# Two mixers of a float32 block: the convolution's two projections ahead of the gated attention's queries and keys

## What is computed

```python
p = h @ w_in                                     # 1024 columns in, 2064 out
gq, gk, gv, gr, glr, ca, cg, sq, sk, sv = jnp.split(p, offsets, axis=-1)
# gated linear attention, 4 heads: scores with a decay per key feature, chunks of 64 and a state
glog = jax.nn.log_sigmoid(glr @ w_gate2 + b_gate) / 16
attn = jnp.einsum('bhid,bhjd,bhijd->bhij', qn, kn, decay)
# convolution group: 256 channels, 31 causal taps, then a norm over the channels and a silu
u = ca * jax.nn.sigmoid(cg)
y = depthwise_conv(u, conv_w) + conv_b
# window attention, 8 query heads, window 128, then one projection of all three groups
return jnp.concatenate([o_gla, o_conv, o_swa], axis=-1) @ w_out
```

## Time and profile before

| | |
|---|---|
| median of 3 runs | 1483.65 us (1483.37 to 1484.98) |
| the profiled execution, its own time | 1483.47 us |
| its span, first to last instruction | 1481.7 us |
| mean granted PE clock | 0.999 |
| PE busy, DVE, ACT, POOL | 98%, 65%, 50%, 6% |
| first mixer, second mixer (start of units 0 to the end of the output projection) | about 682 to 792 us, 1175 to 1284 us |

### The profile page before, as it was taken

The page is one execution under the profiler, slowest core; times in us unless marked ns, Lnnn a source line. Parts: engine busy times, 40 slices in busy tenths (PEclk is TensorE's granted clock), DMA queues, the critical chain, the costliest instruction groups (busy, mean ns, idle before and its releaser), DMA issues. The chain is left out here.

```text
span 1481.7 us, 21669 instructions
## 1 busy us (share of the span) xinstructions
PE 1452.5 (98%) x9016; PEld 1272.4 (86%) x9016; DVE 962.5 (65%) x1163; ACT 737.5 (50%) x936; POOL 86.8 (6%) x106
## 2 busy tenths in 40 slices
PE   7999999999999999999999999999999999999998
PEld 7999999899988788888887888878888898788886
DVE  6867786678774765646776666457565577766644
ACT  5433863555543544445565444444444467544442
POOL 0000000000000000000630000000000035000000
PEclk9999999999999999999999999999999999999999
DMA  7735465666655476555523755557754462366542
GB/s 253 235 115 170 143 198 183 172 190 183 181 190 190 147 245 208 176 187 142 153 90 119 237 181 189 174 168 227 227 185 164 141 181 100 116 211 189 180 162 94
DMA packets 253461, 259.16 MB, mean 175 GB/s; under 512 B 26659, under 2 KB 217524, under 8 KB 253364
## 3 DMA queue, kind: packets, MB, share of 16 engines
q1 hardware_dynamic: 252480, 255.49, 54.5%
q10 hardware_dynamic: 884, 2.28, 0.5%
HBM read 256.69 MB, written 1.05 MB: 174 GB/s over the span
## 5 line engine op out<-in xcount | busy, mean ns | idle before, releaser
L994 DVE TENSOR_TENSOR w_lo<-raw,w_hi 128x2048 fp32r<-128x2048 f32 x240 | 545.9, 2277 | 334.5 <-ACT w_hi L601 334.3
L601 ACT ACTIVATE w_hi<-raw 128x2048 fp32r<-128x2048 f32 x240 | 456.3, 1901 | 346.2 <-PE psm L1668 151.6
L1668 PE MATMUL stream<-a_hi,w_hi 128*128 128x256 f32 x1072 | 306.7, 286 | 2.8 <-DVE a_lo L1013 1.7
L1668 PE MATMUL stream<-a_lo,w_hi 128*128 128x256 f32 x1072 | 303.8, 283 | 0.0
L1668 PE MATMUL stream<-a_hi,w_lo 128*128 128x256 f32 x1072 | 303.8, 283 | 0.0
L1668 PE MATMUL stream<-w_hi,a_hi 128*128 128x512 f32 (+1 forms) x640 | 243.6, 381 | 8.0 <-DVE w_lo L994 5.7
L1668 PE MATMUL stream<-w_hi,a_lo 128*128 128x512 f32 (+1 forms) x640 | 239.2, 374 | 0.0
L1668 PE MATMUL stream<-w_lo,a_hi 128*128 128x512 f32 (+1 forms) x640 | 238.9, 373 | 0.0
L1668 PEld LDWEIGHTS stream<-a_hi,w_hi 128*128 128x128 f32 x1072 | 206.1, 192 | 4.9 <-issue 3.0
L1668 PEld LDWEIGHTS stream<-a_lo,w_hi 128*128 128x128 f32 x1072 | 206.3, 192 | 0.0
L1668 PEld LDWEIGHTS stream<-a_hi,w_lo 128*128 128x128 f32 x1072 | 206.2, 192 | 0.0
(11 more groups left out here) (285 smaller groups left out, 1662.2 us busy)
## 6 DMA issues: line engine op xcount, KB each, us to landing
raw<-in_ffn_w_up SPq DMA_DIRECT2D x136, 512.0 KB, 5.0
raw<-in_ffn_w_down SPq DMA_DIRECT2D x104, 512.0 KB, 4.4
raw<-in_ffn_w_gate SPq DMA_DIRECT2D x88, 512.0 KB, 3.9
raw<-in_w_in SPq DMA_DIRECT2D x80, 512.0 KB, 4.6
raw<-in_w_out SPq DMA_DIRECT2D x24, 512.0 KB, 4.2
raw<-in_w_ret_o SPq DMA_DIRECT2D x8, 512.0 KB, 4.1
raw<-in_w_lru_o SPq DMA_DIRECT2D x8, 512.0 KB, 3.9
diag<-in_conv_diag SPq DMA_DIRECT2D x8, 512.0 KB, 5.8
```

The costliest lines, as they stand in the source:

```text
L601: nc.scalar.activation(w_hi[s][:, :, 0:n], raw[s][:, :, 0:n], ACT.Copy).then_inc(w_hi_ready, 1)
L994: V.tensor_tensor(w_lo[s][:, :, 0:n], raw[s][:, :, 0:n], w_hi[s][:, :, 0:n].bitcast(F32), ALU.subtract).then_inc(w_split, 1)
L1668: return nc.tensor.matmul(dst, lhs, rhs, start=start, stop=stop, skip_group_check=True)
```

## The change

In both mixers, on all engines:

- The weights of units 2, 3 and 4 change places: `ca` is now unit 2, `cg` unit 3, queries and keys unit 4. All three have the same size.
- DVE reads `ca` and `cg` first and makes `up`; then come `qg`, `kg` and `qe`, then `conv(0, 2)` and `read_pair(5)`, and only then the drain of tile 0. `lo(cm + 7)` now stands behind this drain.
- ACT takes the tanh of `cg` before `hi(cm + 6)`, four tap products before `hi(cm + 7)` and ten behind it, ahead of `hi(cm + 8)`.
- POOL makes three additions before the key products and the other 25 behind them.
- PE makes the scores of tile 0 behind the whole unit 5, and those of tile 1 behind the whole unit 6 (before: behind their first halves). Of the 21 taps, 7 stand ahead of the cross scores (before 3), then 2, 4, 4, 3 and 1 (before 2, 4, 4, 4 and 4).

No instruction is added or removed.

```diff
@@ SP
-                for n, col in enumerate((0, 784, 1040, 1808)):
+                for n, col in enumerate((784, 1040, 0, 1808)):
@@ POOL
+                sums(0, FIRST_TAPS)
                 for t in range(TT):
-                    pool.wait_ge(group_evac, g_mix + 3)
+                    pool.wait_ge(group_evac, g_mix + 5)
                     pool.wait_ge(e_ready, TT * l + t + 1)
...
-                for n, (f, tap) in enumerate(SUM_TAPS):
...
+                sums(FIRST_TAPS, len(SUM_TAPS))
@@ ACT
+                act.wait_ge(group_evac, gm + 4)
+                nc.scalar.activation(th2[:, :, :], th2[:, :, :], ACT.Tanh, scale=0.5).then_inc(glu_th, 1)
                 hi(cm + 6)
-                act.wait_ge(group_evac, gm + 5)
-                nc.scalar.activation(th2[:, :, :], th2[:, :, :], ACT.Tanh, scale=0.5).then_inc(glu_th, 1)
+                tap_products(0, FIRST_TAPS)
                 hi(cm + 7)
-                tap_products(0, 8)
+                tap_products(FIRST_TAPS, 14)
                 hi(cm + 8)
-                tap_products(8, 14)
@@ DVE
                 sink_columns()
                 lo(cm + 4)
+                read_pair(2, ca[:, :, :], 0.5)
                 lo(cm + 5)
-                read_pair(3, ca[:, :, :], 0.5)
+                read_pair(3, th2[:, :, :], 1.0)
...
+                lo(cm + 6)
+                dve.wait_ge(unit_used, USED[cm + 4])
...
                 for t in range(TT):
-                    dve.wait_ge(group_evac, gm + 3)
+                    dve.wait_ge(group_evac, gm + 5)
...
-                lo(cm + 6)
...
+                conv(0, 2)
+                read_pair(5, sq2[:, :, :], 1.0)
+                gla_scores(0)
                 lo(cm + 7)
-                gla_scores(0)
-                read_pair(5, sq2[:, :, :], 1.0)
-                conv(0, 2)
                 gla_scores(1)
@@ PE
                 unit(5)
                 first_half(5)
+                second_half(5)
                 gla_scores(0)
-                second_half(5)
                 unit(6)
                 first_half(6)
+                second_half(6)
                 gla_scores(1)
-                second_half(6)
...
-                conv_taps(3)
+                conv_taps(7)
                 psm_ready(PSM_CROSS)
...
-                conv_taps(4)
+                conv_taps(3)
                 pe.wait_ge(group_evac, gm + 9)
```

More of the change, by code:

```diff
@@ L86 @@
 HELD = 3
+FIRST_TAPS = 4
 SHARED = (20, 10)
@@ L549, in _, with sums @@
                 nc.gpsimd.memset(up[:, :, 0:TAPS - 1], 0.0).then_inc(zeroed, 1)
+                def sums(first, to):
+                    for n in range(first, to):
+                        f, tap = SUM_TAPS[n]
+                        pool.wait_ge(tap_product, len(SUM_TAPS) * l + n + 1)
+                        if tap:
+                            if tap > 1:
+                                pool.wait_ge(pool_tap, N_SUMS * l + SUM_AT[n])
+                            nc.gpsimd.tensor_tensor(tap_sum[f], tap_sum[f], tap_ring[:, SUM_AT[n] % RING_N, :],
+                                                    ALU.add).then_inc(pool_tap, 1)
+                sums(0, FIRST_TAPS)
                 for t in range(TT):
-                    pool.wait_ge(group_evac, g_mix + 3)
+                    pool.wait_ge(group_evac, g_mix + 5)
                     pool.wait_ge(e_ready, TT * l + t + 1)
@@ L1550, in _ @@
                                        op0=ALU.min, op1=ALU.subtract).then_inc(ps7_free, 1)
[L1551 to L1554, removed]
                 sink_columns()
                 lo(cm + 4)
+                read_pair(2, ca[:, :, :], 0.5)
                 lo(cm + 5)
-                read_pair(3, ca[:, :, :], 0.5)
+                read_pair(3, th2[:, :, :], 1.0)
+                dve.wait_ge(zeroed, 2 * l + 2)
+                dve.wait_ge(group_evac, gm + 3)
+                dve.wait_ge(glu_th, l + 1)
+                V.scalar_tensor_tensor(out=up[:, :, TAPS - 1:TAPS - 1 + T], in0=th2[:, :, :], scalar=1.0,
+                                       in1=ca[:, :, :], op0=ALU.add, op1=ALU.mult).then_inc(up_ready, 1)
+                lo(cm + 6)
+                dve.wait_ge(unit_used, USED[cm + 4])
+                V.scalar_tensor_tensor(out=qg[:, :], in0=bank(4)[:, 0:T], scalar=GDK ** -0.5, in1=rb[:, :],
+                                       op0=ALU.mult, op1=ALU.mult)
+                V.tensor_tensor(kg[:, :], bank(4)[:, T:2 * T], rb[:, :], ALU.mult).then_inc(group_evac, 1)
                 for t in range(TT):
-                    dve.wait_ge(group_evac, gm + 3)
+                    dve.wait_ge(group_evac, gm + 5)
                     dve.wait_ge(e_ready, TT * l + t + 1)
```

## The result

| | before | after |
|---|---|---|
| median | 1483.65 us (7 runs, 1483.36 to 1484.98) | 1490.31 us (7 runs, 1488.91 to 1492.16) |
| the profiled execution, its own time | 1483.47 us | 1490.38 us |
| its span | 1481.7 us | 1488.6 us |
| mean granted PE clock | 0.999 | 0.997 |

The ratio is 1.004, with an interval of 1.003 to 1.005: slower by 6.7 us, where 4.0 were forecast, and past the upper end of the range (1489.4).

The account below looks back on a forecast made before the run. PE was taken to bound the kernel: unchanged work plus waits. Per mixer, +1.8 taps, +0.65 new wait, -0.47 old wait, +0.0 to +0.2 second drain make 2.0; 4.0 in all on 1483.65 us gives 1487.7, range 1485.8 to 1489.4.

Parts of the forecast that it names:

- The chain: From PE's cross scores through ACT, POOL, PE and DVE to `yc`: 36 us whatever PE does, so delay reaches the mean.
- S: How much later the cross scores, and so the convolution's mean, start in each mixer; forecast 1.7 to 2.5 us, chance 0.69.
- Rival 2: The mean does not hang on the cross scores: -0.9 to +0.4 us, 1482.7 to 1484.1 us; chance 0.07.
- S = 2.0: Cross scores at about 735.1 instead of 733.13: +1.8 taps, +0.65 new wait, -0.47 old wait, +0.0 to +0.2 second drain.
- The new wait for `ek`: Before PE's scores of tile 0: PE arrives at 721.2, POOL's key product at 721.8, a wait of 0.65 us.
- The old wait of 0.40: PE's wait for the drain of tile 0, before the scores of tile 1: gone, 0.47 us with its restart.
- The drain of tile 1: DVE's second drain, done at 734.7 or 735.2, about when PE reaches the cross scores: +0.0 to +0.2 us.
- The taps: Seven instead of three ahead of PE's cross scores: four more cost 1.8 us per mixer.
- Turns of DVE and POOL: DVE instructions with two SBUF inputs and POOL's SBUF reads exclude each other: a sum of 4.0 us, 2.4 without turns.
- The sum: Cross scores 2.0 us later per mixer, 4.0 in both: 1487.7 us; PE waits about 1.8 us more inside the chain.
- The range: 1485.8 to 1489.4 us for the whole kernel, from delays of 1.1 to 2.9 us per mixer.

Follow-up runs that it names:

- b_taps7: The kernel before with only PE's taps dealt out as in the change (7 ahead of the cross scores, then 2, 4, 4, 3, 1): 1490.90 us, ratio 1.0039.
- a_again: The changed kernel run once more, unedited: 1489.55 us, ratio 1.0037.
- a_keys_first: The changed kernel with POOL's two key products put back ahead of all 28 additions: 1497.06 us, ratio 1.0085.
- a_fill_first: The changed kernel with two throwaway PE products in the first pause (for `b_lo`), none in the second (for `yc`): 1487.93 us, ratio 1.0030.
- a_taps3: The changed kernel with PE's old split of the taps (3 ahead of the cross scores, then 2, 4, 4, 4, 4): 1487.07 us, ratio 1.0022.
- a_conv_early: The changed kernel with DVE's `conv(4, 9)` ahead of its wait for the tanh of `gr`: 1486.46 us, ratio 1.0018.

## Why the prediction was wrong, step by step

**The chain: right.** "If the cross scores start S later, the mean starts S later" held in the changed kernel (1.94 and 1.97) and with the taps undone (1.61 and 1.60). Filling PE's pauses did not move the mean, and shortening the chain on ACT and DVE did. Rival 2 is out.

**S = 2.0: right, and its parts.** The new wait for `ek` was put at 0.65 and is 0.66. The old wait of 0.40 is gone, and `vs` kept its 0.56. The drain of tile 1 was put at "734.7 or 735.2"; less the 1.33 of the launch it ends at 734.7. The taps were put at 1.8 for four; seven take 3.26 against 1.53 for three, 1.73. What the sum did not say is that the two causes lie beside each other: leaving either out gives back only 0.25 to 0.35 us per mixer (S = 1.70 and 1.60 instead of 1.95).

**Turns of DVE and POOL: right.** The Trainium skill (SBUF — State Buffer, Who interferes with whom) gives the exclusive turns, and says in the same place that the form `tensor_scalar` can fall under them; DVE's first two taps are of that form and took about 2.45 us each beside key products of POOL. The prediction had them wait their turn too, to 722.1 and 724.6; less the 1.33 of the launch they ended at 721.9 and 724.3.

**The sum: here it failed.** It says "In PE's waits it shows as follows: the chain is S later and PE has 1.8 us of taps less inside it, so PE waits about 1.8 us more than the 0.17 of before, part at the first `b_lo` and part at `yc`". The pauses came nearly as written: 0.63 + 1.16 = 1.79, 1.62 more than the 0.17. But they were priced only as waiting. The step that failed is the first one, "So the time is PE's work, which the change leaves as it is (same matmuls, same sizes), plus PE's waits, and only these can move": the same matmuls take longer at a lower clock, and the sum has no term for that. No step asked what two such pauses close together do to PE's clock.

In the profiled execution it fell to the 1.2 GHz level for 3.4 us behind them, in one mixer, at 1.66 us. In b_taps7 it fell in both. The four profiled executions with this pair of pauses (the changed kernel, a_again, b_taps7, a_keys_first) have it in eight places, and the clock fell behind four of them. Over all runs, 5 of the 17 of the changed kernel and b_taps7 have a clock of 0.998 or more, against 69 of 69 of the seven kernels in which one of the two pauses or both are gone (all but a_keys_first). Filling the pauses took the median from 1490.31 to 1488.15 with S unchanged; filling the first alone gave 1487.93; and two executions of the changed kernel took 1487.6 and 1487.8, that of 1487.8 profiled without a fall. With the fall kept away the change costs 4.1 us on either chip, against 4.0 forecast. So the term that was missing is 0, 1.7 or 3.4 us, most often more than zero.

**The range: too narrow for the same reason.** Its upper end came from S near 3 and nothing else. With S = 2.0 and two falls it would have been 1487.7 + 3.3 = 1491.0. The launch adds up to 1.3 more in an execution, as in the profiled one. The largest time measured, 1492.16, is 1483.47 + 3.9 + 3.3 + 1.3 = 1492.0 by these parts; that this one run was made up so is argued, as it has no trace.

**What stays open.** Why the clock falls behind the two pauses in one execution and not in another with the same pauses, and why in one mixer and not the other. In the changed kernel the second pause alone is not enough, as a_fill_first shows; the first alone was not tried, though the like of it (0.56 us for a later `b_lo`) stands in every trace with the clock at 1.00. What makes a pair or a pause bring a fall is not known. The pair of 0.57 and 1.34 us in a_taps3 brought none, and of the two pauses of 3.19 us in a_keys_first one did and one did not. That the fall comes more often than not is read from the clock of 12 runs.

## What to carry to other kernels

Price a wait of the engine that bounds the kernel twice: as waiting, and as what it may do to the clock behind it; two pauses of 0.63 and 1.16 us side by side brought, more often than not, a fall of 1.7 us, nearly as much again as the waits themselves. Before moving a bounding engine's work ahead of a point, ask which other engine's chain starts at that point, since work put ahead of it delays the chain's end in full, while what is saved inside turns into a wait. And look for the gain at the chain's own idle places: four products and seven taps moved into 2 to 3 us of idleness on ACT and DVE gave 1482.07 us, ratio 0.9983 [0.9974, 0.9992], better than both kernels.

## What the runs showed of the hardware that was not expected

- PE pauses of 0.63 and 1.16 us with three matmuls between them were followed, in four of eight places of the profiled executions, by about 3.4 us at a granted 0.50 to 0.56. A pause of 1.17 or 1.18 us without the first one was not (a_fill_first, a_conv_early), and neither were 0.57 and 1.34 us with three taps between them (a_taps3), in the profiled executions. A pause of 3.18 us was, for 6.9 us, and the same pause of 3.19 us in the other mixer of that execution was not.
- The same kernel with the same pauses to 0.01 us was seen with and without the fall.
- The launch differs between executions: the granted clock was 0.50 from 16.7 to 20.1 us in one, from 18.8 to 22.2 in another, and 1.00 through both stretches in a_again; unit 0 of the first mixer stood at 687.51, 688.84 and 688.06. So full clock in these stretches did not bring the earliest unit 0.
- A DVE tap of 0.41 us lasted 2.45 us beside a POOL product of 2.4 us.
